# Three of four root rows spread through DRAM instead of through TensorE

## The reference, cut to what matters

```
x = x + 0.5 * swiglu_ffn(rms_norm(x, ffn1_norm))       # norm 0
x = first mixer of rms_norm(x, mix_norm)               # norm 1
x = x + 0.5 * swiglu_ffn(rms_norm(x, ffn2_norm))       # norm 2
f = swiglu(rmsnorm(x, ffn1_pre_g_2))                   # norm 3
rms_norm(x, g) = x * rsqrt(mean(x * x, over channels) + 1e-6) * g
```

## Time and profile before

| | |
|---|---|
| median of 3 runs | 1110.36 us (1109.59 to 1111.8) |
| profiled execution, its own time | 1111.69 us |
| its span, first to last instruction | 1109.9 us |
| PE busy | 1100.8 us, 99% of the span |
| DVE busy | 744.9 us, 67% |
| ACT busy | 557.3 us, 50% |
| POOL busy | 50.3 us, 5% |
| mean granted TensorE clock | 0.998 of full speed |

### The profile page before, as it was taken

The page is one execution under the profiler, slowest core; times in us unless marked ns, Lnnn a source line. Parts: engine busy times, 40 slices in busy tenths (PEclk is TensorE's granted clock), DMA queues, the critical chain, the costliest instruction groups (busy, mean ns, idle before and its releaser), DMA issues.

```text
span 1109.9 us, 19623 instructions
## 1 busy us (share of the span) xinstructions
PE 1100.8 (99%) x8422; PEld 1041.4 (94%) x8422; DVE 744.9 (67%) x858; ACT 557.3 (50%) x737; POOL 50.3 (5%) x60
## 2 busy tenths in 40 slices
PE   9999999999999999999999999999999999999998
PEld 8999999988989999999999998889988987999986
DVE  7766665788977676665476675566858657666652
ACT  7544443657464454443364455445746446444441
POOL 0000000200000000000020000010201001000000
PEclk9999999999999999999999999999999999999999
DMA  8866656734465475656576575549355536766641
GB/s 311 267 191 189 209 158 177 251 112 125 130 186 169 149 256 186 197 184 209 153 266 213 161 253 175 184 121 352 119 161 188 192 114 187 232 192 189 202 139 38
DMA packets 112422, 207.74 MB, mean 187 GB/s; under 512 B 8912, under 2 KB 18768, under 8 KB 112208
## 3 DMA queue, kind: packets, MB, share of 16 engines
q1 hardware_dynamic: 109968, 198.53, 56.0%
q0 software_dynamic: 2080, 7.87, 2.0%
q10 hardware_dynamic: 288, 0.10, 0.0%
HBM read 205.42 MB, written 1.05 MB: 186 GB/s over the span
## 4 chain that ended last, share of the span: by engine, by line
PE 92%; DVE 5%; issue 1%; DMA 1%; ACT 1%; POOL 0%; DVEq 0%; POOLq 0%; SPq 0%; ACTq 0%
PE pair L469 90%; DVE w_lo L1498 2%; PE pair L473 2%; DMA stage<-in_ffn_w_up 1%; DVE work L1842 0%; DMA stage<-in_ffn_w_gate 0%; DVE top L1840 0%; DVE x L1687 0%; ACT w_hi L1084 0%; DVE xr L1524 0%; DVE nmax_a L1723 0%; DVE big L1717 0%; DVE ga L1741 0%; DVE dm L1871 0%; DVE den L1876 0%
## 5 line engine op out<-in xcount | busy, mean ns | idle before, releaser
L1498 DVE TENSOR_TENSOR w_lo<-stage,w_hi 128x1024 fp32r<-128x1024 f32 (+1 forms) x382 | 452.6, 1209 | 207.6 <-ACT w_hi L1084 206.3
L1084 ACT CAST w_hi<-stage 128x1024 fp32r<-128x1024 f32 (+1 forms) x382 | 383.8, 1030 | 241.6 <-PE pair L469 229.3
L469 PE MATMUL pair<-h_hi,w_hi 128*128 128x256 f32 x1760 | 490.9, 279 | 0.2 <-DVE w_lo L1498 0.2
L469 PE MATMUL pair<-h_lo,w_hi 128*128 128x256 f32 x1760 | 487.4, 277 | 0.0
L469 PE MATMUL pair<-h_hi,w_lo 128*128 128x256 f32 x1760 | 487.1, 277 | 0.0
L469 PEld LDWEIGHTS pair<-h_hi,w_hi 128*128 128x128 f32 x1760 | 331.7, 189 | 4.4 <-issue 3.0
L469 PEld LDWEIGHTS pair<-h_lo,w_hi 128*128 128x128 f32 x1760 | 331.4, 188 | 0.2
L469 PEld LDWEIGHTS pair<-h_hi,w_lo 128*128 128x128 f32 x1760 | 331.0, 188 | 0.0
L469 PE MATMUL pair<-f_hi,w_lo 128*128 128x256 f32 x352 | 97.2, 276 | 0.0
L469 PE MATMUL pair<-f_hi,w_hi 128*128 128x256 f32 x352 | 97.2, 276 | 0.0
L469 PE MATMUL pair<-f_lo,w_hi 128*128 128x256 f32 x352 | 97.2, 276 | 0.0
(11 more groups left out here) (310 smaller groups left out, 1122.5 us busy)
## 6 DMA issues: line engine op xcount, KB each, us to landing
stage<-in_ffn_w_down SPq DMA_DIRECT2D x88, 512.0 KB, 3.8
stage<-in_ffn_w_gate SPq DMA_DIRECT2D x86, 512.0 KB, 4.4
stage<-in_ffn_w_up SPq DMA_DIRECT2D x83, 512.0 KB, 4.6
stage<-in_w_in SPq DMA_DIRECT2D x52, 512.0 KB, 4.4
stage<-in_w_out SPq DMA_DIRECT2D x16, 512.0 KB, 4.2
stage<-in_xa_wkv SPq DMA_DIRECT2D x16, 512.0 KB, 5.1
stage<-in_xa_wq SPq DMA_DIRECT2D x8, 512.0 KB, 4.3
stage<-in_xa_wo SPq DMA_DIRECT2D x8, 512.0 KB, 6.3
```

The costliest lines, as they stand in the source:

```text
L469: return e.matmul(o, l, r, start=start, stop=stop, skip_group_check=True)
L1084: e.copy(m.w_hi[u % PLACES][:, plan.place(u)], m.stage[u % STAGES][:, 0:w]).then_inc(s.hi, 1)
L1498: e.tensor_tensor(m.w_lo[slot][:, plan.place(u)], m.stage[u % STAGES][:, 0:w], m.w_hi[slot][:, plan.place(u)].bitcast(F32), ALU.subtract). ...
```

## The change

For norms 1, 2 and 3 the diagonal, the product and the copy are gone. POOL, after its two root instructions, waits for both, sends the two columns to a DRAM tensor of 256 numbers (two DMAs, each 128 pieces of 4 bytes), waits until both have landed, and reads the 256 numbers back to all 128 partitions (one DMA, 1 KB to each). The readers of the row wait for the semaphore of that last DMA. Norm 0 keeps the old way. In the feed-forward parts the wait for the row now stands behind `lo_to(last + 6)` and not ahead of it.

```diff
@@ tensor: ffn_by_columns, mixer1
-            if j == at + 1:
-                spread_roots(i)
+            if n == 0 and j == at + 1:
+                spread_roots(0)
@@
-        spread_roots(1)
@@ scalar: ffn_by_columns, mixer1
-                root_rows((0, 2, 3)[n])
+                if n == 0:
+                    root_rows(0)
@@
-                e.wait_ge(s.rB, 4)
+                e.wait_ge(s.rrow, 48)
@@
-        root_rows(1)
@@ vector: ffn_by_columns
-                diagonal(i)
+                if n == 0:
+                    diagonal(0)
                 lo_to(F + (7 if n == 0 else 6))
-                e.wait_ge(s.rB, i + 1)
             if n or b:
                 lo_to(last + 6)
+            if b == 0 and n == 0:
+                e.wait_ge(s.rB, 1)
+            elif b == 0:
+                e.wait_ge(s.rrow, 16 * i)
@@ vector: post_part
+        if p == 0:
+            e.wait_ge(s.rcol, 4 * T)
@@ vector: mixer1
-        diagonal(1)
@@
-        e.wait_ge(s.rB, 2)
+        e.wait_ge(s.rrow, 16)
@@ gpsimd: column_roots
+        if i:
+            e.wait_ge(s.rcol, T * (i + 1))
+            for t in range(T):
+                e.dma_start(d["roots"].rearrange("(t p n) -> t p n", t=T, n=1)[t], m.rB[i][:, S + t:S + t + 1]).then_inc(s.rkept, 16)
+            e.wait_ge(s.rkept, 16 * T * i)
+            e.dma_start(m.rB[i][:, 0:S], d["roots"].partition_broadcast(P)).then_inc(s.rrow, 16)
@@ kernel
+    d["roots"] = nc.dram_tensor("roots", (S,), F32, kind="Internal").ap()
```

More of the change, by code:

```diff
@@ L92 @@
     hi lo used half pow zero pow2 one
-    uhi ulo xT sqT fold ssum stp var rcol diag sprd rB gr dev xbk xrow
+    uhi ulo xT sqT fold ssum stp var rcol diag sprd rB rkept rrow gr dev xbk xrow
     sq ms rt xr tr nhi nlo xup
```

## The result

The changed kernel took 1128.7 us (median of 4 runs, 1124.04 to 1134.72) against 1109.97 for the kernel before (4 runs, 1108.29 to 1111.8): ratio 1.016, 95% interval 1.013 to 1.0191. It is slower by 1.6%. The forecast was 1109.1 us, the range ended at 1111.8, and "slower by over 0.2%" had a chance of 0.10.

A forecast was written before the change was run, and what follows sets the result against it. TensorE, busy 99% of the span, was taken to bound the kernel. Three removed products of 0.43 us gave 1.29 us less, with nothing counted elsewhere: from the median 1110.36 to 1109.1 us, range 1106.8 to 1111.8.

The forecast's parts named there:

- What bounds the kernel: Whole span: TensorE, busy 99%, sets the time, and all three places of the change count in full.
- The product that goes: Norms 1, 2 and 3: each removed diagonal product frees 0.43 us of TensorE's stream, 1.29 us in all.
- The time by which the row must be there: Norm 2: row needed by 393.1 us, expected at about 389, room of 4 us; norm 3 the same 180.5 us later.
- The roots: POOL at norm 2: roots start at 381.55 us, take 2.01 us beside w_lo, done at 383.56.
- The stores: POOL to DRAM behind norm 2's roots: second store issued at 384.15 us, landing in 2.3 us, at 386.45.
- The load back: Behind norm 2's stores: load of 1 KB to each partition takes 2.3 us, row there at about 389 us.
- Rival 2, the late row: Norms 2 and 3: transfers wait among weight loads, row misses 393.1 us; 3.2 us slower, 1113.6 us, chance 0.12.
- The rule weighed: Both transfers through DRAM: 1.8 us more each from DRAM latency under load, row at about 392.6 us, still early.
- Rival 1, the clock fall at 229: Low clock from 228.93 to 232.35 us may not come, saving 1.6 us: 1107.5 us, chance 0.18.
- Norm 1: Row lands near 204 us, first use at 218.47 us: 14 us of room.
- The later weights: DVE's w_lo behind the row in the second block: lateness made up in idle time (17.89 of 23 us busy).

The follow-up runs named there:

- e1: Changed kernel without the stores, the row loaded from a constant right behind the roots: 1109.07 us against 1111.23 for the kernel before, ratio 0.9985.
- e2: Changed kernel with root columns transposed in blocks by DVE, each store 4 pieces of 128 bytes: 1113.61 us, ratio 1.003.
- e5: Changed kernel without stores, row from a constant, twelve more root instructions on POOL ahead of the load at norms 2 and 3: 1119.45 us, ratio 1.0093.
- e4: Changed kernel with one store in place of two at each norm, row from a constant: 1127.2 us, single run.
- e12: Changed kernel with the stores' 4-byte pieces 512 bytes apart in DRAM, row from a constant: 1111.86 us, single run.
- e14: The changed kernel run again with an empty line ahead of it: 1129.26 us, single run.
- e3: Kernel before, diagonal product kept, plus pairs of the same stores at 226.5 us and behind norm 2 and 3's roots, needed by nobody: 1109.78 us, ratio 0.9992.
- e13: The changed kernel as it is, run again with its trace: 1134.86 us, single run.

## Why the prediction was wrong, point by point

- **What bounds the kernel: right.** TensorE's stream decides, and norms 2 and 3 lie on it. Each wait there shows up whole in the later starts of all products behind it.
- **The product that goes: right.** 1.3 us were counted, and e1, which has nothing else of the change on the path, gained 1.7 us by its ratio, with an interval of 0.4 to 3.0. In the traces one product is worth about 0.4 us (e1).
- **The time by which the row must be there: right.** 393.1 against roots at 381.55 is 11.5 us behind their start, and I took the row to be there 7.5 us behind it. e2's row came about 12.8 behind and TensorE waited 0.4 at norm 2; e5's at 14.7 gave 2.3; the changed kernel's at 15.9 gave 3.6. These lie on one line of slope one that begins at 12.4: the room was 0.9 us larger than worked out.
- **The roots: mis-sized by 0.6 us.** I took 2.01, from norm 1's row; beside w_lo they took 2.60 at all three norms, against 1.08 with DVE still. Two pauses of 0.28 us on POOL, ahead of the first store and ahead of the load, were not counted either.
- **The stores: this is the step that failed.** "The stores have no row of their own kind [...] I take 2.3, as amount and queue are nearest to that row." At norm 2 the last one took 8.83 us, 6.5 more than the 2.3, and at norms 3 and 1 it took 9.85 and 10.25. The bounds that I gave, up to 5.6 us, were those of large transfers and bounded nothing: amount isn't what such a store costs. Its cost is in adjacent 4-byte writes to DRAM. With the same packets 64 or 512 bytes apart it is 4.2 to 4.8, with the same packets into SBUF 4.5 to 5.2, with 4 pieces of 128 bytes 3.0 to 3.8.
- **The load back: mis-sized too.** Taken at 2.3 from one row of its shape, whose load was issued at 190 us. I read that row and the output's stores as "also beside the weight loads"; neither is. The output's stores go at 1098 us and later, behind the last weights, and at 190 us no DMA moved. The DMA view of the kernel before has three more loads of 128 KB on POOL's queue, which I left out, two of them issued 1.1 and 1.9 us behind the one that I took. The window of before ahead of 191 us, then the loads:

```profile
189.00:191.00 2.00, 2.00 (x10) 1.63 (x10) 1.97 (x5) 1.58 (x4) 0.51 (x1) 1.00 0.00 0
```

```profile
causal<-in_consts POOLq DMA_DIRECT2D x1, 128.0 KB, 3.9
...
w_mq<-in_w_mq POOLq DMA_DIRECT2D x1, 128.0 KB, 3.3
w_mk<-in_w_mk POOLq DMA_DIRECT2D x1, 128.0 KB, 3.1
```

  It took 3.29 and 3.85 us behind the stores at norms 2 and 3, and 6.2 and 6.9 without them (e1), where it goes out earlier, among more weight loads. By itself it would have fitted (e1).
- **Rival 2, the late row, was the mechanism** with its condition right as a sum ("both transfers must take more than about 4.5 us each": the load took less, 3.29, but with the store's 8.83 it is over twice 4.5). Its chance of 0.12 and its price of 3.2 us were too small. The waits alone were 8.8. Not priced at all was the low clock that follows a stop, 4.1 us here. The slower pace, up to 7 us in a run, was not in the prediction either, though its own trace had it from 320 to 380 us.
- **The rule weighed** gave a row at 392.6, by an estimate from the Trainium skill's page "DMA: Bandwidth & Descriptors", section "Latency and other measured facts". The measurement decides: with 2 us for DRAM under high load, once for each transfer, the estimate is 4.1 us, and it reaches neither the last stores (8.8 to 10.3 us) nor the load of e1 (5.6 to 6.9). But it pointed the right way, and I gave it no weight in the chances.
- **Rival 1, the clock fall at 229:** it stayed in the changed kernel's three traces, and was gone in e4, e5 and e12. It has no part in the loss of the profiled execution. In e14 the low clock there lasted 10.2 us and not 3.4, behind the longer wait for ikT.
- **Norm 1: the row was early enough, as predicted.** It was there at 216.3 us, and its first use was at 220.2 us. What I didn't look at is what stands behind the row's load in POOL's program: two more roots for the indexer, which now wait for the stores. TensorE waited 0.9 to 2.4 us for them in the changed kernel's three traces.
- **The later weights.** I counted on them being made in time, and they were, but the stores do hold up other packets. The weight loads issued beside them took 8.5 us at norm 2 and 9.8 at norm 3:

```profile
q1 hardware_dynamic: 1252, 2.40, 75.1%
...
stage<-in_ffn_w_up SPq DMA_DIRECT2D x3, 512.0 KB, 8.5
...
roots<-r_low POOLq DMA_DIRECT2D x2, 0.5 KB, 7.6
```

(Changed kernel, DMA view of 383 to 398 us; over the whole span these loads have a median of 4.6.) In a window of it, 389 to 391.5, the DMA engines are as busy as before and move a quarter as much, first after, then before:

```profile
389.00:391.50 2.50, 2.50 (x24) 2.50 (x23) 0.00 (x0) 0.00 (x0) 0.00 (x0) 1.00 1.10 89
```

```profile
389.00:391.50 2.50, 2.50 (x25) 2.50 (x24) 0.62 (x1) 2.50 (x3) 0.00 (x0) 1.00 0.95 364
```

e3 shows that the reserve in the stage buffers covers this. As long as nobody waits for the row it costs nothing that can be measured. It is not the stores' alone: the load of one row to all partitions does it too where weight loads are issued beside it (e1, 7.5 to 9.1 us).

What stays open: what brings on the slow pace, and what in the write of neighbouring pieces is slow. That their being less than 64 bytes apart in DRAM matters is shown, and in e3 the time passes behind the last packet; by what means it acts is not shown.

## What to carry to other kernels

The price of a small transfer goes by its pieces and where they lie more than by its bytes: 512 bytes took 3 to 4 us or 9 to 10 here. Where the trace has no row of the same pieces, the range must be far wider than the rows of larger ones, and a step with a fixed date should be judged by the late end. Writing a column of 4-byte numbers side by side to DRAM is a slow way to turn it; with the column transposed in blocks first the stores landed in 3 to 4 us in the median, and a single hop from SBUF to SBUF in 3 to 5. And a stop of an engine that is otherwise never idle costs more than its length: count the clock, and look at the pace behind it, before a product of 0.43 us is traded for a chain with a deadline.

## What the runs showed of the hardware that was not expected

- TensorE has two paces at full granted clock, 177 and 170 matmuls of 256 columns started in 20 us (0.113 and 0.118 us apart), each kept over stretches of 60 to 180 us. The kernel before shows the slow one too, from 320 to 380 us, and the pace differs between executions of the same kernel (profiled execution, e13, e14).
- A store of 128 adjacent 4-byte pieces to DRAM landed in 6.3 to 11.8 us beside weight loads and in 5.5 and 7.5 in the quiet place (e3), from POOL's queue and from ACT's; 64 or 512 bytes apart it was 3.8 to 5.2. In the quiet place the second landing came over 5 us behind the last packet, with no other DMA under way. While such stores were under way the weight loads took 8.5 to 9.8 us in the median in place of 4.6.
- The load of one 1 KB row to 128 partitions, issued right behind the roots, took 6.8 and 6.9 us at norms 2 and 3 where 128 different rows took 4.4 and 4.2 (single executions), and 5.6 both ways at norm 1; issued later, it took 3.1 to 3.3.
- Two root instructions on POOL took 2.60 us beside DVE's w_lo and 1.08 us with DVE idle.
